# Choosing experts tile by tile, and transposes between the halves of an out-projection product, in a two-layer mixture-of-experts block

## The reference

```python
x = layer_norm(ALPHA * x + g1 * o_x, ln1_g[l], ln1_b[l])       # o_x = mixture @ w_out[l]; the context in the same way
hx = (x * (1 + sc2) + sh2).reshape(b_ * s_, d_)
...
g_logit = hf @ w_rg + b_rg                                      # 4 groups
g_val, g_idx = lax.top_k(g_logit, 1)
e_logit = ...take_along_axis(e_logit, g_idx[:, :, None], axis=1)[:, 0]
e_val, e_idx = lax.top_k(e_logit, TOP_K)                        # 2 of the group's 8 experts
gates = p_group[:, None] * jax.nn.softmax(e_val, axis=-1)
...                                                             # rows are gathered into blocks by expert
ys = (silu(xb @ w1[e]) * (xb @ w3[e])) @ w2[e]
```

## Time and profile before

| | |
|---|---|
| Time before, median of 3 runs | 3073.74 us (3071.37 to 3075.64) |
| Profiled execution, span | 3074.4 us; the page gives no time around the span |
| PE busy | 2743.3 us, 89% |
| DVE busy | 1062.8 us, 35% |
| ACT, POOL busy | 459.4 us, 15%; 316.7 us, 10% |
| Out-projection to first gather, layer 0 | 1385.8 to 1524.4 us |
| Out-projection to first gather, layer 1 | 2329.4 to 2432.5 us |

### The profile page before, as it was taken

The page is one execution under the profiler, slowest core; times in us unless marked ns, Lnnn a source line. Parts: engine busy times, 40 slices in busy tenths (PEclk is TensorE's granted clock), DMA queues, the critical chain, the costliest instruction groups (busy, mean ns, idle before and its releaser), DMA issues.

```text
span 3074.4 us, 33083 instructions
## 1 busy us (share of the span) xinstructions
PE 2743.3 (89%) x11436; PEld 1248.1 (41%) x11436; DVE 1062.8 (35%) x2065; ACT 459.4 (15%) x874; POOL 316.7 (10%) x445
## 2 busy tenths in 40 slices
PE   7999999999998999999699977886999688999772
PEld 3444444444444456564433322233555333333221
DVE  5998960330003042454531111115454511111104
ACT  3111130100111010451101100002151000111000
POOL 0101011000000000001122211110000111221110
PEclk9999999999998999999799998998999799999886
DMA  6665341221220311002699999974201899779993
GB/s 229 211 198 185 110 179 57 99 82 65 72 82 1 120 55 39 17 1 71 242 347 372 380 393 392 392 291 182 99 1 50 289 390 381 258 271 367 394 352 132
DMA packets 272217, 603.12 MB, mean 196 GB/s; under 512 B 18436, under 2 KB 43332, under 8 KB 272000
## 3 DMA queue, kind: packets, MB, share of 16 engines
q1 hardware_dynamic: 256864, 580.70, 51.9%
q0 software_dynamic: 15264, 21.24, 2.0%
HBM read 743.04 MB, written 29.20 MB: 251 GB/s over the span
## 4 chain that ended last, share of the span: by engine, by line
PE 71%; SPq 12%; DMA 8%; DVE 5%; issue 2%; ACT 2%; POOL 0%; POOLq 0%; DVEq 0%; ACTq 0%
PE psum L1022 11%; PE psum L1410 11%; PE psum L1109 11%; SPq L657 10%; PE psum L1244 9%; PE psum L1080 7%; DMA arena<-in_w 6%; PE psum L1348 4%; PE psum L1432 4%; PE psum L1291 3%; PE psum L1280 2%; PE psum L1007 1%; PE psum L1130 1%; PE psum L1303 1%; PE psum L1397 1%
## 5 line engine op out<-in xcount | busy, mean ns | idle before, releaser
L1410 PE MATMUL psum<-arena 128*64 128x512 f32 x2656 | 648.5, 634 | 121.1 <-DMA arena<-in_w 119.5
L1410 PEld LDWEIGHTS psum<-arena 128*64 128x64 f32 x2656 | 196.5, 144 | 453.6 <-issue 448.4
L1022 PE MATMUL psum<-arena 128*128 128x512 f32 x768 | 341.2, 600 | 2.6 <-ACTq L754 2.6
L1109 PE MATMUL psum<-arena 128*128 128x512 f32 x768 | 329.9, 592 | 0.8 <-ACT arena L733 0.8
L1432 PE MATMUL psum<-arena 128*64 128x512 f32 x1328 | 301.2, 597 | 0.3 <-issue 0.3
L1509 DVE SCALAR_TENSOR_TENSOR arena<-arena 128x512 f32<-128x512 f32 x451 | 300.1, 743 | 0.0
L1244 PE MATMUL psum<-arena 128*128 128x512 f32 (+1 forms) x800 | 287.7, 519 | 5.4 <-ACT arena L820 5.4
L1080 PE MATMUL psum<-arena 128*128 128x512 f32 x512 | 224.4, 601 | 5.2 <-POOL arena L2182 4.4
L1109 PEld LDWEIGHTS psum<-arena 128*128 128x128 f32 x768 | 145.8, 190 | 184.2 <-issue 183.2
L1022 PEld LDWEIGHTS psum<-arena 128*128 128x128 f32 x768 | 143.4, 191 | 177.1 <-issue 174.3
L1244 PEld LDWEIGHTS psum<-arena 128*128 128x128 f32 x800 | 151.1, 191 | 128.6 <-issue 113.1
(11 more groups left out here) (279 smaller groups left out, 2039.2 us busy)
## 6 DMA issues: line engine op xcount, KB each, us to landing
arena<-in_w SPq DMA_DIRECT2D x261, 2048.0 KB
arena<-in_w_ada SPq DMA_DIRECT2D x48, 1024.0 KB, 5.2
arena<-in_conv_w_in SPq DMA_DIRECT2D x24, 1024.0 KB
arena<-in_ret_w_in SPq DMA_DIRECT2D x12, 2048.0 KB, 7.9
arena<-in_w_in SPq DMA_DIRECT2D x8, 2048.0 KB, 9.2
arena<-moe_out SPq DMA_DIRECT2D x10, 1024.0 KB, 10.4
arena<-in_conv_w_out SPq DMA_DIRECT2D x4, 2048.0 KB, 11.9
arena<-in_ret_w_out SPq DMA_DIRECT2D x4, 2048.0 KB, 7.8
```

Of the source, the lines that this page charges most:

```text
L1022: m = pe.matmul(bank(b + c), w[:, k, c * P:(c + 1) * P], c_hT[:, k, :], start=(k == 0), stop=(k == KD - 1))
L1109: m = pe.matmul(bank(4 * (n % 2) + j), l_, r_, start=(k == 0), stop=(k == KD - 1))
L1410: m = pe.matmul(bank(2 * s)[part], m_xsT[s][:, at:at + SB], m_w[s][j][:, k, :], start=(k == 0), stop=(k == KD - 1))
```

## The change

PE: the transposes of tile t-1 now stand between the two halves of tile t, and the logits of tile t-1 behind its second half. The logits of tile nt-2 close the loop, and transposes and logits of tile nt-1 follow as before.

DVE: `add_product` now does one half at a time. Between the halves stand the copy of the turned tile before and the scaling of the rows of the tile before. The choice of experts is a function `route(t0, t1)`. It is called for one tile after each of the tiles 1 to nt-2, and for the last two tiles together behind everything else. ACT waits as before for marks that only the last call gives. ACT's, POOL's and SP's programs are unchanged.

```diff
--- before.py
+++ after.py
@@ -1343,6 +1343,8 @@
                     if t >= 2:
                         pe.wait_ge(sem("ob_x"), past("ob_x", l) + 2 * (t - 1))
                     for hf in range(2):
+                        if hf == 1 and t >= 1:
+                            mod_transposes(2 * l + 1, t - 1)
                         for k in range(KD):
                             y = b_att[:, k] if k < 4 else b_cv[:, k - 4] if k < 6 else b_gmT[:, k - 6]
                             m = pe.matmul(bank(2 * (t % 2) + hf), y[:, t * P:(t + 1) * P],
@@ -1350,11 +1352,8 @@
                                           start=(k == 0), stop=(k == KD - 1))
                         m.then_inc(sem("ob_mm"), 1)
                     if t >= 1:
-                        mod_transposes(2 * l + 1, t - 1)
-                    if t >= 2:
                         pe.wait_ge(sem("wr"), past("wr", l) + 16)
-                        logits(t - 2)
-                logits(nt - 2)
+                        logits(t - 1)
                 mod_transposes(2 * l + 1, nt - 1)
                 logits(nt - 1)
                 pe.wait_ge(sem("rt_M"), past("rt_M", l) + 1)
@@ -1653,14 +1652,13 @@
                 r_gate(h - 1)
                 r_norm(h)
             r_gate(RH - 1)
-            def finish_rows(q, tiles, first, mod_q, free=None):
+            def finish_rows(q, tiles, first, mod_q, free=None, route=None):
                 nt = len(tiles)
                 def stats_of(i_):
-                    first(i_, tiles[i_])
                     for hf in range(2):
                         link(dve.bn_stats(stats[:, 100 + 12 * i_ + 6 * hf:106 + 12 * i_ + 6 * hf],
                                           xr[:, tiles[i_], hf * CW:(hf + 1) * CW]))
@@ -1694,14 +1692,20 @@
                 dve.wait_ge(sem("row_w"), 32 * (q + 1))
                 dve.wait_ge(sem("fin_x"), past_full(q) + (TX if q % 2 == 0 else nt))
                 for i_ in range(nt):
-                    stats_of(i_)
                     if free:
+                        first(i_, tiles[i_], 0)
                         if i_ >= 1:
                             mod_copy(mod_q, i_ - 1)
+                        if 1 <= i_ < nt - 1:
+                            rows(i_ - 1)
+                        first(i_, tiles[i_], 1)
+                        stats_of(i_)
                         norm(i_)
                         if 1 <= i_ < nt - 1:
-                            rows(i_ - 1)
+                            route(i_ - 1, i_)
                         continue
+                    first(i_, tiles[i_])
+                    stats_of(i_)
                     if mod_q == 2 and i_ < 3:
                         norm(i_)
                     elif i_ >= (4 if mod_q == 2 else 1):
@@ -1925,19 +1929,14 @@
                     link(dve.scalar_tensor_tensor(out=scale, in0=scale, scalar=1.0, in1=b_ln[0],
                                                   op0=ALU.add, op1=ALU.mult))
-                def add_product(i_, t):
-                    for hf in range(2):
-                        dve.wait_ge(sem("ob_mm"), past("ob_mm", l) + 2 * i_ + hf + 1)
-                        cols = slice(hf * CW, (hf + 1) * CW)
-                        dve.tensor_tensor(b_tmp[:, cols], bank(2 * (t % 2) + hf), b_mod[3 * (t >= TX)][:, cols],
-                                          ALU.mult).then_inc(sem("ob_x"), 1)
-                        dve.wait_ge(sem("ob_x"), past("ob_x", l) + 2 * i_ + hf + 1)
-                        link(dve.scalar_tensor_tensor(out=xr[:, t, cols], in0=xr[:, t, cols], scalar=ALPHA,
-                                                      in1=b_tmp[:, cols], op0=ALU.mult, op1=ALU.add))
-                finish_rows(2 * l, tiles, add_product, 2 * l + 1,
-                            lambda: dve.wait_ge(sem("ob_mm"), past("ob_mm", l) + 2 * nt))
+                def add_product(i_, t, hf):
+                    dve.wait_ge(sem("ob_mm"), past("ob_mm", l) + 2 * i_ + hf + 1)
+                    cols = slice(hf * CW, (hf + 1) * CW)
+                    dve.tensor_tensor(b_tmp[:, cols], bank(2 * (t % 2) + hf), b_mod[3 * (t >= TX)][:, cols],
+                                      ALU.mult).then_inc(sem("ob_x"), 1)
+                    dve.wait_ge(sem("ob_x"), past("ob_x", l) + 2 * i_ + hf + 1)
+                    link(dve.scalar_tensor_tensor(out=xr[:, t, cols], in0=xr[:, t, cols], scalar=ALPHA,
+                                                  in1=b_tmp[:, cols], op0=ALU.mult, op1=ALU.add))
                 def arr(o, *dims):
@@ -1963,36 +1962,50 @@
                 be = mem(g_s + 272, 4)
                 iota = mem(TAB + T_I, 120)
-                def first_of(dst, idx, vals, top, width):
-                    it = iota[:, 0:width].unsqueeze(1).to_broadcast([P, nt, width])
-                    link(dve.tensor_tensor(dst, vals, over(top, nt, width), ALU.is_equal))
+                def first_of(dst, idx, vals, top, n, width):
+                    it = iota[:, 0:width].unsqueeze(1).to_broadcast([P, n, width])
+                    link(dve.tensor_tensor(dst, vals, over(top, n, width), ALU.is_equal))
                     link(dve.scalar_tensor_tensor(out=dst, in0=dst, scalar=-1000.0, in1=it, op0=ALU.mult, op1=ALU.add))
                     link(dve.tensor_reduce(idx, dst, AX.X, ALU.min))
-                    link(dve.tensor_tensor(dst, dst, over(idx, nt, width), ALU.is_equal))
-                dve.wait_ge(sem("lg_mm"), past("lg_mm", l) + nt)
-                rb = mem(SMALL + V_RB + (NG + E) * l, NG + E).unsqueeze(1).to_broadcast([P, nt, NG + E])
-                link(dve.tensor_tensor(lg, bank(6, (NG + E) * nt).rearrange("p (t e) -> p t e", t=nt), rb, ALU.add))
-                link(dve.tensor_reduce(gmax, lg[:, :, 0:NG], AX.X, ALU.max))
-                dve.tensor_tensor(ge, lg[:, :, 0:NG], over(gmax, nt, NG), ALU.subtract).then_inc(sem("rt_dve"), 1)
-                first_of(goh, gi, lg[:, :, 0:NG], gmax, NG)
-                link(dve.tensor_scalar(gc, goh, -1.0, BIG, ALU.add, ALU.mult))
-                for t in range(nt):
-                    link(dve.tensor_tensor(el[:, t, :].rearrange("p (g e) -> p g e", g=NG),
-                                           lg[:, t, NG:NG + E].rearrange("p (g e) -> p g e", g=NG),
-                                           gc[:, t, :].unsqueeze(2).to_broadcast([P, NG, EPG]), ALU.add))
-                link(dve.tensor_reduce(m1, el, AX.X, ALU.max))
-                first_of(oh1, i1, el, m1, E)
-                link(dve.scalar_tensor_tensor(out=el, in0=oh1, scalar=-3 * BIG, in1=el, op0=ALU.mult, op1=ALU.add))
-                link(dve.tensor_reduce(m2, el, AX.X, ALU.max))
-                first_of(oh2, i2, el, m2, E)
-                dve.tensor_tensor(ed, m2, m1, ALU.subtract).then_inc(sem("rt_dve"), 1)
-                link(dve.tensor_tensor(M, oh1, oh2, ALU.add))
-                link(dve.memset(before[:, 0, :], 0.0))
-                for t in range(nt - 1):
-                    link(dve.tensor_tensor(before[:, t + 1, :], before[:, t, :], M[:, t, :], ALU.add))
+                    link(dve.tensor_tensor(dst, dst, over(idx, n, width), ALU.is_equal))
+                def route(t0, t1):
+                    n, r = t1 - t0, slice(t0, t1)
+                    dve.wait_ge(sem("lg_mm"), past("lg_mm", l) + t1)
+                    rb = mem(SMALL + V_RB + (NG + E) * l, NG + E).unsqueeze(1).to_broadcast([P, n, NG + E])
+                    logit = bank(6, (NG + E) * n, (NG + E) * t0).rearrange("p (t e) -> p t e", t=n)
+                    group = lg[:, r, 0:NG]
+                    link(dve.tensor_tensor(lg[:, r, :], logit, rb, ALU.add))
+                    link(dve.tensor_reduce(gmax[:, r], group, AX.X, ALU.max))
+                    last_ge = dve.tensor_tensor(ge[:, r, :], group, over(gmax[:, r], n, NG), ALU.subtract)
+                    if t1 == nt:
+                        last_ge.then_inc(sem("rt_dve"), 1)
+                    first_of(goh[:, r, :], gi[:, r], group, gmax[:, r], n, NG)
+                    link(dve.tensor_scalar(gc[:, r, :], goh[:, r, :], -1.0, BIG, ALU.add, ALU.mult))
+                    for t in range(t0, t1):
+                        link(dve.tensor_tensor(el[:, t, :].rearrange("p (g e) -> p g e", g=NG),
+                                               lg[:, t, NG:NG + E].rearrange("p (g e) -> p g e", g=NG),
+                                               gc[:, t, :].unsqueeze(2).to_broadcast([P, NG, EPG]), ALU.add))
+                    link(dve.tensor_reduce(m1[:, r], el[:, r, :], AX.X, ALU.max))
+                    first_of(oh1[:, r, :], i1[:, r], el[:, r, :], m1[:, r], n, E)
+                    link(dve.scalar_tensor_tensor(out=el[:, r, :], in0=oh1[:, r, :], scalar=-3 * BIG, in1=el[:, r, :],
+                                                  op0=ALU.mult, op1=ALU.add))
+                    link(dve.tensor_reduce(m2[:, r], el[:, r, :], AX.X, ALU.max))
+                    first_of(oh2[:, r, :], i2[:, r], el[:, r, :], m2[:, r], n, E)
```

(11 more changed lines are left out.)

## The result

The kernel after takes 3080.99 us, median of 20 runs (3075.81 to 3088.81); the kernel before took 3073.88, median of 20 on the same chip (3066.9 to 3077.75). The ratio is 1.0024 [1.0017, 1.0032]: 7 us slower. The forecast was 3076.4 with a range up to 3081.0, so the time lies at the very top of the range, and above the 3073 to 3077.5 that the forecast gave for its own sum.

The account below looks back on a forecast made before the run. PE sets the out-projection stretch, then the chain through expert choice to the first gather; TensorE then waits for weights. Layer 0 +4.4 and layer 1 -1.7 gave +2.7 us, median 3073.7 to 3076.4; range 3069.5 to 3081.

Parts of the forecast that it names:

- The stall: Layer 0 out-projection: PE waits before tile 0's transposes until VectorE has normalised that tile, +4.85 us; none in layer 1.
- The clock behind it: Layer 0, the half after PE's idle gap runs partly at 1.2 GHz: +1.7 us, bounds 0 and 2.7.
- The first rival: Nothing paid for the gap's clock, last transposes at full rate, gathers land as before: 3069.5 us; chance 0.17, half-effect included.
- The turns in front of E and the tail: One more transposes and logits before the last out-projection product ends, +2.58 us; last transposes then end 6.47 behind it.
- The choice: Choosing experts for two tiles instead of all at the end saves 3.5 us in layer 0, 1.7 in layer 1.
- that rival: Last choice of experts: GpSimd's additions no longer block VectorE, saving up to 2.1 us per layer, 3072.2; chance 0.05.
- the fourth rival: Middle tiles' one-tile choice of experts does not fit under PE's products: +8 us on top, 3085; chance 0.05.
- The gathers: Each layer's first gather, nearer the weight stream, lands after 6.1 us: +2.5 in layer 0, +0.9 in layer 1.
- The third rival: First gathers land only with the weight stream's end, 8.0 us in both layers: +6.5 in all, 3080.2; chance 0.15.
- The sum at the landed gather: Shift of the first gather's landing: +4.4 us in layer 0, -1.7 in layer 1, together +2.7.
- 1:1 passage: Expert stages behind each layer's first gather: any shift of its landing reaches the kernel's end in full, here +2.7 us.

Follow-up runs that it names:

- the kernel with that turn late: Kernel after, but in layer 0 tile 0's transposes go back behind both halves of tile 1, its logits between tile 2's halves; ratio 0.9986, again 0.999.
- the one with that turn alone: Kernel before, with only tile 0's transposes in layer 0 moved between the halves of tile 1; ratio 1.002.
- the turns alone: Kernel after with its transposes between the halves, but all tiles' experts chosen in one set behind the last logits; 3084.67 us, ratio 1.0028.
- the rows early: Kernel after, with the scaling of the last tile but one's rows moved ahead of the last tile's copy, so GpSimd's additions end sooner; ratio 0.9998.
- the choice alone: TensorE's order of the kernel before; middle tiles' experts chosen one by one under the products, the last three tiles together; ratio 0.9994.
- both repairs: Kernel after with layer 0's tile 0 transposes behind tile 1's second half and the last-but-one tile's rows scaled ahead of the last copy; 3064.7 us, ratio 0.9968.
- the eleven unused products: Kernel after, with eleven extra 128x512 matmuls, results unused, ahead of tile 0's transposes in layer 0; ratio 1.0038.
- five unused products: Kernel after, with five extra 128x512 matmuls, results unused, ahead of tile 0's transposes in layer 0; ratio 0.9998, again 1.0004.

## Why the prediction was partly wrong

*The stall: right.* Forecast 4.85 us of idle PE; the profiles have 5.01, 4.33 and 4.62. It isn't there in layer 1, as said, and the kernel with that turn late and the one with that turn alone show it from both sides as the cause of the loss.

*The clock behind it: mechanism right, term too small.* +1.7 was taken for the half alone; measured 2.2 to 2.6. The half was sized well (+1.4 to +1.8). The transposes of tile 0, which come first after the gap, were left at full rate, though the prediction itself had the last tile's at 1.77 after some 3 us of idleness. They cost some 0.85 more. E moved by 9.7 to 10.4 where 9.1 was forecast. The first rival, in which neither this clock nor the stream at the gathers costs anything, failed on both.

*The turns in front of E and the tail: right.* E in layer 1 moved by 2.65 (2.58 forecast); T stands 6.65 behind E in layer 0 and 5.8 to 6.2 in layer 1 (6.47). T moved by +6.2 to +6.9 (forecast +5.4, the difference being for the most part the clock) and by -1.1 to -1.5 (-0.9).

*The choice: right, a little small.* From T to the ranks, 16.84 became 12.92 in layer 0, -3.9 (forecast -3.5), and 15.02 became 12.92 in layer 1, -2.1 (-1.7). The forecast left out that the blocked operation is now a later one: the third of the choice before in layer 0 and the fourth in layer 1, now the fifth in both, so two small operations and one, at some 0.2 each, have moved ahead of the block. The operation blocked by GpSimd stayed, so that rival failed. In the middle the choice took 4.8 us, under the products: the fourth rival failed.

*The gathers: right.* 6.5 and 5.9 in place of the 6.1 assumed, against 3.58 and 5.17 before (3.62 and 5.57 in its second profile); the kernel with two loads behind the gather shows the stream as the cause. The third rival failed on its own condition: landing at 8.0, decided from 7.8 on. That its 3080.2 lies near the measured time is chance, since none of its extra 3.8 us appeared.

*The sum at the landed gather: right in total, by luck in part.* Forecast +4.4 and -1.7, together +2.7. Measured +5.9 and -2.7 in the first profile, +5.3 and -3.1 in the second, +5.2 and -3.2 in the third: together 3.2, 2.2 and 2.0. Each layer is off by about a microsecond or more (layer 0 by the clock, layer 1 by tail and choice), and the errors cancel.

*The step that failed:* "I let a shift of the first gather's landing pass 1:1 to the end". It carried the +2.7 at X to the end unchanged. What the runs showed in its place: +3.2, +2.2 and +2.0 at X, but +3.5, +6.5 and +2.5 (mean 4.2) from the first product to the end of the three profiles, and +7.1, +6.5 and +3.0 (mean 5.5) in the three timed comparisons.

A part of the difference is seen in the profiles: at P, one product later, the net is +4.6, +4.2 and +2.2. The whole of what came between X and P, +1.5, +2.0 and +0.2, is the first expert product of each layer. It runs at a granted clock of 0.77 and 0.73 in the first profile of after and takes 8.9 to 9.1 us in layer 0 (8.6 before), and 9.5, 10.0 and 8.4 in layer 1 (8.6 and 8.5 before). A longer wait for the gather suggests itself as the cause, but in layer 1 the wait hardly grew. PE's timeline there, before:

```profile
2424.49 1.53 PE L1382 MATMUL psum<-arena 128*64 128x96 f32 x16
2432.60 1.09 PE L1397 MATMUL psum<-arena 128*128 128x128 f32 x4 [6.57 <-DMA arena<-moe_in,arena]
2434.51 8.58 PE L1410 MATMUL psum<-arena 128*64 128x512 f32 x32 [0.83 <-issue]
```

And after:

```profile
2430.63 2.82 PE L1381 MATMUL psum<-arena 128*64 128x96 f32 x16
2439.25 1.08 PE L1396 MATMUL psum<-arena 128*128 128x128 f32 x4 [5.80 <-DMA arena<-moe_in,arena]
2441.17 9.52 PE L1409 MATMUL psum<-arena 128*64 128x512 f32 x32 [0.83 <-issue]
```

From the start of the first row to that of the second it is 8.1 us before (8.5 in the second profile) and 8.6, 8.8 and 8.6 after, and behind these three the product took 9.52, 10.03 and 8.44. In layer 0 the idle time grew from 4.1 to 7.0 us, for 0.3 to 0.5 more; but with the turns alone 4.58 us of it were followed by 9.68, and with the rows early 6.62 by 8.46. So the length of this wait does not set the product's time, and what does stays open.

Behind P, -1.1, +2.3 and +0.3 us in the three profiles change their sign from profile to profile, with the clock of layer 1's attention and the expert stages, which differ as much between profiles of one kernel.

So of the 5.5 us, 2.5 are the sum of the prediction at X (mean), about 1.2 the first products, and 1.8 are not settled: a true loss in the expert stages or scatter. The other kernels don't show a general failure of the 1:1 passage. In the ten runs of changed kernels other than after that leave the order of the weights alone, the timed median moved against before by what X moved, both layers together, within 2 us in nine (the turn alone +7.5 for +7.4, the turns alone +9.0 for +7.2, the choice alone -1.5 for -1.3, the late turn -4.3 and -5.6 for -4.7, both repairs -10.3 for -8.4), and missed it by 5.9 only with the eleven unused products. The kernel after itself lies 3.9, 4.3 and 1.0 us above what its X says, and why is not known. Where weight loads were moved behind the gather, the time lies 6.7 and 4.1 us above what X says.

## What to carry to other kernels

When a turn is moved forward in an engine's order, look first at the first tile: there the other engines have not yet found their lead, and one early turn cost more than the rest of the change saved. Price a new idle gap of TensorE as the wait plus the slower work behind it, every instruction of it counted, the small ones too. When a chain ends in a DMA, ask what else is in the queues at its new time: an issue made earlier, as in the choice alone, can be paid back by a landing made later.

## What was unexpected in the hardware

- A gap of 4.3 to 5.0 us cost 2.2 to 2.6 us on top; filling it with unused products gave that back. In a stretch set by PE, five unused products brought E forward by 2.3 us against idleness (the times, 1.0004 against 1.0013 on one chip, have overlapping intervals and don't show it).
- A layer's first gather takes 2.4 to 6.6 us to land in these kernels, depending on the weights behind which it is issued. It takes 3.54 and 2.37 (layer 0 and 1) with one of the three loads of the second expert ahead of it, 5.80 and 4.19 with two (in the kernel with both repairs), 6.5 and 5.9 with all three (in the kernel after).
- The attention of layer 1 runs at a clock of 0.98 in some profiles and 0.94 in others, 3.4 us apart for identical instructions.
